# Moving whole parts of the modulation products to other places in a four-layer transformer kernel

## The reference, cut to what matters

```python
mod = jax.nn.silu(c) @ w_mod[l] + b_mod[l]           # (1024,) @ (1024, 6144)
sh1, sc1, g1, sh2, sc2, g2 = jnp.split(mod[:, None, :], 6, axis=-1)
h = x * (1 + sc1) + sh1
x = _layer_norm(ALPHA * x + g1 * mixers(h), ...)
h = x * (1 + sc2) + sh2
x = _layer_norm(ALPHA * x + g2 * mlp(h), ...)
```

## Time and profile before

| | us |
|---|---|
| median of 3 runs | 3222.01 (3219.78 to 3222.47) |
| the profiled execution's own time | 3220.32 |
| its span, first to last instruction | 3219.0 |
| PE busy in the span | 3019.1 (94%) |
| share of PE in the chain that ended last | 87% |
| mean granted clock of TensorE | 0.966 |

### The profile page before, as it was taken

One profiled execution on the slowest core, in us unless ns is written; L12 is line 12 of the kernel. 1 busy time (PEld: TensorE's weight loads), 2 busy tenths in 40 slices (PEclk: granted clock), 3 DMA queues, 4 the chain that ended last, 5 costly groups with the idle time before them and its releaser, 6 DMA issues.

```text
span 3219.0 us, 41567 instructions
## 1 busy us (share of the span) xinstructions
PE 3019.1 (94%) x17128; PEld 2308.4 (72%) x17128; DVE 1418.2 (44%) x2184; ACT 1072.9 (33%) x1807; POOL 313.1 (10%) x334
## 2 busy tenths in 40 slices
PE   5989999999999988999999998997889999899998
PEld 3766657788888866766667776775567888678886
DVE  2556542423233345654444445536734444344443
ACT  3235441412122242553422335212533323342222
POOL 1012220300000030221201002000310000110000
PEclk7999999999999999999999999998989999889999
DMA  6313134222212122103343322422322232222322
GB/s 236 94 58 105 34 119 150 86 99 85 66 60 65 58 77 69 60 14 127 134 150 98 103 87 79 165 94 92 99 85 92 94 96 92 67 66 92 98 92 79
DMA packets 83876, 299.08 MB, mean 93 GB/s; under 512 B 9479, under 2 KB 11783, under 8 KB 83432
## 3 DMA queue, kind: packets, MB, share of 16 engines
q1 hardware_dynamic: 79200, 286.30, 27.2%
q10 hardware_dynamic: 4488, 10.12, 0.9%
HBM read 294.29 MB, written 2.10 MB: 92 GB/s over the span
## 4 chain that ended last, share of the span: by engine, by line
PE 87%; DVE 5%; ACT 4%; issue 2%; DMA 1%; POOL 1%; ACTq 0%; DVEq 0%; POOLq 0%
PE bank L592 42%; PE bank L596 21%; PE bank L1013 4%; PE bank L455 3%; PE bank L1030 3%; PE bank L1074 2%; PE bank L2682 2%; PE bank L1828 1%; PE bank L1566 1%; DMA t<-in_mod 1%; PE bank L1450 1%; PE bank L1022 1%; ACT t L1288 1%; ACT t L843 1%; ACT t L1112 1%
## 5 line engine op out<-in xcount | busy, mean ns | idle before, releaser
L592 PE MATMUL bank<-t 128*128 128x512 f32 (+1 forms) x6432 | 1757.3, 374 | 26.5 <-DVE t L2326 11.1
L592 PEld LDWEIGHTS bank<-t 128*128 128x128 f32 x6432 | 1113.0, 189 | 297.1 <-issue 69.1
L596 PE MATMUL bank<-t 128*128 128x512 f32 (+1 forms) x3216 | 1070.7, 372 | 5.9 <-POOL t L852 5.7
L596 PEld LDWEIGHTS bank<-t 128*128 128x128 f32 x3216 | 556.8, 189 | 127.4 <-POOL t L852 12.0
L486 ACT ACTIVATE t<-t 128x1024 fp32r<-128x1024 f32 x350 | 366.3, 1050 | 558.4 <-PE bank L596 497.5
L496 DVE TENSOR_TENSOR t<-t 128x1024 fp32r<-128x1024 f32 x350 | 430.5, 1234 | 262.4 <-ACT t L486 258.8
L609 DVE SCALAR_TENSOR_TENSOR t<-bank,t 128x512 f32<-128x512 f32 x192 | 129.8, 693 | 511.0 <-PE bank L596 484.2
L933 DVE TENSOR_TENSOR t<-t 128x512 f32<-128x512 f32 (+1 forms) x128 | 98.4, 769 | 335.8 <-ACT t L913 335.8
L913 ACT ACTIVATE t<-bank 128x512 f32<-128x512 f32 (+1 forms) x128 | 83.3, 651 | 418.7 <-PE bank L596 418.7
L1214 POOL TENSOR_SCALAR t<-t 128x768 f32<-128x768 f32 (+3 forms) x160 | 125.7, 788 | 576.3 <-DVE t L1182 576.3
L455 PE MATMUL bank<-t 128*32 128x256 f32 x1536 | 128.9, 414 | 33.7 <-DMA t<-in_mod 23.5
(11 more groups left out here) (289 smaller groups left out, 2281.4 us busy)
## 6 DMA issues: line engine op xcount, KB each, us to landing
t<-in_mod SPq DMA_DIRECT2D x192, 512.0 KB, 4.3
t<-in_l0fc SPq DMA_DIRECT2D x64, 512.0 KB, 3.5
t<-in_l1fc SPq DMA_DIRECT2D x64, 512.0 KB, 3.5
t<-in_s0fc SPq DMA_DIRECT2D x64, 512.0 KB, 3.5
t<-in_s1fc SPq DMA_DIRECT2D x64, 512.0 KB, 3.5
t<-in_mixin SPq DMA_DIRECT2D x24, 512.0 KB, 3.5
t<-in_l0in SPq DMA_DIRECT2D x12, 512.0 KB, 3.6
t<-in_l1in SPq DMA_DIRECT2D x12, 512.0 KB, 3.5
```

Of the source, the lines that this page charges most:

```text
L592: pe.matmul(acc.ap[:, o:o + m], w[:, ws], Hh[:, k, o:o + m], start=k == 0 and w is hi, stop=False)
L596: ins = pe.matmul(acc.ap[:, o:o + m], hi[:, ws], Hl[:, k, o:o + m], start=False, stop=k == NK - 1)
```

## The change

Parts are now placed whole, and at other places:

- Around the norms ln10, ln20, ln11, s0h and pool one part each: 2 tiles before the last pair of sums, 2 before `pe_picks`, 1 before `pe_spread`, 3 behind it.
- In the first two units of the attentions of layers 0 and 1 one part (5, 1 and 2 tiles), and of the differential attention one (5 and 3). In layers 0 and 1 the pieces begin in unit 2 instead of 0.
- Behind the four transforms between layers 1 and 2 one part, at the new mark "transformed".
- In the output projection of layer 0 one mod tile goes behind each weight tile instead of two; in the MLPs of layers 0 and 1 and the output product of the third layer there are none; in the third layer's input products 16 over 20 tiles instead of one behind each, and the row of four is gone. Layer 0's units 4 to 12 have 8 instead of 16.
- The eight tiles of part (3, 5) now stand in a row ahead of the first fc2 tile of the last MLP, where `t.need(L, 5)` places them.
- Turns come earlier in several places (`finish_part`). In the pool layer the first three slices of h are made before the queues' entries up to "pool out".

Counted by part, before and after: (0,3) attention units 4 to 8, now units 0 and 1; (1,3) output projection, now ln10; (1,4) MLP, now ln20; (1,5) MLP, now projections of layer 1; (2,0) these projections, now units 0 and 1 of attention 1; (2,4) MLP, now ln11; (2,5) MLP, now behind the transforms; (3,2) input products and the row of four, now units 0 and 1 of the differential attention; (3,3) that attention, now s0h; (3,4) that attention, now pool; (3,5) output product, now the last MLP.

```diff
+    def spaced(self, n, i, count, upto):
+        self.fill(n * (i + 1) // count - n * i // count, upto)
+
+    def gap(self, tag, counts, upto):
+        assert not any(counts) or not self.pending and self.parts and not self.parts[-1][2], tag
+        for i, n in enumerate(counts):
+            self.fill(n, upto)
+            self.mark(("gap", tag, i))
+        assert sum(counts) in (0, NK), tag
...
-def mlp_order(t, name, L, upto):
+def mlp_order(t, name, L, n, upto, after, counts):
...
-            if m % 4 != 3:
-                t.fill(1, upto)
+            t.spaced(n, 16 * q + m, 64, upto)
...
+    t.finish_part()
     t.mark((name, "end"))
+    t.gap(after, counts, min(upto + 1, 3))
+
+GAP, NO_GAP = (2, 2, 1, 3), (0, 0, 0, 0)
...
-    todo = [(0, x) for x in pair_pieces(l, 0)]
+    todo = [(2, x) for x in pair_pieces(l, 0)]
...
-    mods = ((4, 9, 8), (28, 32, 8)) if l else ((4, 13, 16), (20, 25, 8), (38, 48, 16))
+    mods = ((6, 9, 8), (28, 32, 8)) if l else ((6, 11, 8), (20, 25, 8), (38, 48, 16))
...
+        if u == 1:
+            t.fill(1, l + 1)
         t.mark((f"att{l}", u, "mid"))
         piece(u)
+        if u < 2:
+            t.fill((5, 2)[u], l + 1)
...
-        t.fill(1 if l else 2, l + 1)
+        t.fill(1, l + 1)
+    t.finish_part()
     t.mark((name, "ln1"))
-    mlp_order(t, name, l, l + 1)
+    t.gap(f"ln1{l}", GAP, l + 1)
+    mlp_order(t, name, l, 0, l + 1, f"ln2{l}", NO_GAP if l else GAP)
...
+    t.fill(8, 3)
+    t.mark("transformed")
...
-        t.fill(1, 3)
+        t.spaced(16, n, 20, 3)
...
+    t.finish_part()
     for u in range(16):
-        t.fill(1, 3)
+        if u < 2:
+            t.fill((5, 3)[u], 3)
...
-        t.fill(1, 3)
-    mlp_order(t, "s0", 2, 3)
+    t.gap("s0h", GAP, 3)
+    mlp_order(t, "s0", 2, 0, 3, "pool", GAP)
...
-    mlp_order(t, "s1", 3, 4)
+    t.gap("s1h", NO_GAP, 3)
+    mlp_order(t, "s1", 3, 0, 4, "final", NO_GAP)
...
             if pair == 3:
+                pe_tiles(("gap", N.tag, 0))
             pe_sums(N, pair)
...
+        pe_tiles(("gap", N.tag, 1))
         PEQ.wait_ge(*ps[2].after(("sums", N.tag)))
...
+        pe_tiles(("gap", N.tag, 2))
         PEQ.wait_ge(*at("dve_scales", N.tag))
...
+        pe_tiles(("gap", N.tag, 3))
...
             pe_transform(3)
+            pe_tiles("transformed")
...
             act_transformed(3)
+            act_tiles("transformed")
...
         act_norm_end(N)
+        act_second_h(N, L, 1, work, Hh, range(0, 3))
         act_tiles("pool out")
         act_tiles(("pool", 0))
-        act_second_h(N, L, 1, work, Hh, range(0, 6))
+        act_second_h(N, L, 1, work, Hh, range(3, 6))
...
-        dve_tiles("pool out")
...
         dve_norm_end(N)
+        dve_second_h(N, work, range(0, 3))
         dve_tiles(("pool", 0))
-        dve_second_h(N, work, range(0, 6))
+        dve_second_h(N, work, range(3, 6))
```

More of the change, by code:

```diff
@@ L236, in mlp_order @@
             t.tile((name + "fc2", 8 * q + m))
-            if m % 4 != 3:
-                t.fill(1, upto)
+            t.spaced(n, 16 * q + 8 + m, 64, upto)
+    t.finish_part()
     t.mark((name, "end"))
+    t.gap(after, counts, min(upto + 1, 3))
+GAP, NO_GAP = (2, 2, 1, 3), (0, 0, 0, 0)
 def pair_pieces(l, p):
@@ L285, in first_order @@
         piece(u)
+        if u == 1:
+            t.fill(1, l + 1)
         t.mark((f"att{l}", u, "mid"))
         piece(u)
+        if u < 2:
+            t.fill((5, 2)[u], l + 1)
         for a, b, n in mods:
             if a <= u < b:
-                t.fill(n * (u + 1 - a) // (b - a) - n * (u - a) // (b - a), l + 1)
+                t.spaced(n, u - a, b - a, l + 1)
         if u == 8 * nb - 1:
@@ L669, in pe_norm_step @@
         for pair in ({3: (0,), 5: (1,), 7: (2, 3)} if N.centered else {2: (0,), 4: (1,), 6: (2,), 7: (3,)}).get(m, ()):
+            if pair == 3:
+                pe_tiles(("gap", N.tag, 0))
             pe_sums(N, pair)
```

## The result

| | before | changed |
|---|---|---|
| median of 20 runs each, us | 3220.79 (3215.87 to 3223.15) | 3227.98 (3218.11 to 3237.67) |
| ratio to before, 95% interval | 1 | 1.0023 (1.0014 to 1.0031) |
| profiled execution, us (span) | 3220.32 (3219.0) | 3219.33 (3218.0) |
| mean granted clock | 0.966 | 0.976 |
| PE busy, us | 3019.1 | 3013.4 |

The forecast was 3202, the range 3188 to 3214. It took 3228.67, close to the median, and most readings here are from it.

A forecast was written before the change was run, and what follows sets the result against it. PE bounds the kernel (87% of the wait chain), with mod-tile loads pacing work in pauses. Terms -42.0 - 5.4 + 9.9 + 5.8 + 0.4 + 0.2 + 14 = -17.1, clock 3 more: -20.1, so 3202 us; range 3188 to 3214.

The forecast's parts named there:

- attention 0: Layer 0's attention: unit 2 starts 4.0 us earlier, eight tiles leaving -4.0, four pieces coming in +2.6; net -5.4, between -9 and 0.
- the other places: ln10 +1.8, ln20 +1.7, attention 1 +5.8, ln11 +2.9, transforms +0.2, differential attention +0.4, pool +2.1, last MLP +14 us.
- the clock: Pauses and products behind them: tiles keeping the clock full could return 15 us; 3 taken because load waits leave pauses.
- What went out: Mod tiles leaving busy stretches, 0.77 us each in the MLPs, third-layer output and input products; with layer 0's output projection and row, 42.0.
- a tile's load in a pause: Parts in pauses, three buffers: fourth tile starts 4.3 us after the first; a lone load lands 3.56 after its issue.
- the last MLP: Eight tiles in a row before fc2 end at 11.1 us, then copy, turn and low clock: +14, between +6.2 and +18.
- behind the transforms: Eight tiles from 1980.8 end at 1990.6, before 1991.85: +0.2 us, +3 if a load is late.
- item 3: Rival, chance 0.13: loads land 1 us later at 12 waits, +12, 3214; or removed tiles worth only 0.5 each, 3212.
- Item 4: Rival, chance 0.07: ring turns pauses into load waits, landings 7.79 not 3.56, +50, 3252; decides from 1.7 us later per landing.
- items 1: The forecast itself, chance 0.60: loads of 3.56 us pace each part, 3202 us (3196 to 3208).
- Item 2: Rival, chance 0.20: more work in each pause keeps the clock up, 12 of the 15 us come back, 3193.
- Attention 1: Layer 1's attention: first tile waits for condition vectors, units 0 and 1 cost +3.2, pieces elsewhere +2.6; +5.8, between -3 and +9.

The follow-up runs named there:

- again: Second profile and comparison of the unaltered changed kernel: profiled 3228.67 us, median 3226.93 (9 runs), ratio 1.0023 to the kernel before.
- first profile: First profiled execution of the changed kernel, nothing else altered: 3219.33 us, against 3220.32 for the kernel before.
- the best kernel: Changed kernel plus fourth buffer in two stretches, last MLP's part spread, buffers lent at ln10 and behind the transforms: 3188.20 us, ratio 0.9898 to before.

## Why the prediction was wrong

By the rows of the table: the two MLPs, the output projection, the input products, the row of four and the output product with s0h were to give 40.6, attention 0 5.4, the other places to cost 28.9, and the clock to give 3: -20.1. In *again* they gave 37.3 and 2.8, the others cost 50.0, and the prologue gave 1.4: +8.5.

**What went out was right but for 3.3 us.** A mod tile between weight tiles was 0.77 by the earlier trace rows; the two MLPs gave 11.5 and 10.8 for 16, so 0.72 and 0.68. The kernel without loads gives the same (11.6 and 10.6), so this is PE's own time.

**The step that failed is a tile's load in a pause**: "4.3 from a tile's start to the start of the tile three behind it", with its 3.56 for a landing. From the first tile of a part to its fourth it took, in us:

| | first profile | *again* |
|---|---|---|
| attention 0; ln20 | 4.3; 4.2 | 4.3; 4.3 |
| attention 1; differential attention | 4.6; 4.8 | 4.6; 4.6 |
| transforms; last MLP | 5.0; 5.0 | 4.9; 5.0 |
| pool; s0h | 4.7; 6.1 | 5.5; 5.0 |
| ln11; ln10 | 6.0; 5.9 | 5.4; 7.2 |

It held in attention 0 and at ln20. In these two and in attention 1 the fourth tile's load landed 3.4 to 3.6 us after its issue, in the others 3.9 to 6.4. It failed in three ways.

1. *A full ring was taken for granted.* It is full at ln20, where the weight tiles just before stand without mod tiles, and there the forecast held (+1.7 against 1.5 and 2.1). At ln10 and ln11 the last tile of the part before is done right ahead of the pause, so that the load into the third buffer is issued only 1.0 to 1.2 us ahead of the part's first tile: the third tile waits, then the fourth. That is +5.3 and +6.8 at ln10 where 1.8 was forecast, and 5.7 and 4.9 at ln11 for 2.9. With three buffers lent ln10 costs 0.6 to 0.7.
2. *A round of loads was taken as quicker than it is.* A lone load lands 3.4 to 3.6 us after its issue, but a burst sets free three buffers within a microsecond, and the loads then land 1.3 to 2.5 us behind one another. In attention 0 and the last MLP the forecast had put 1.3 between them; behind the transforms it had left that out. In the last MLP and behind the transforms a weight tile's load was also still in flight, so that the first of the round landed 4.2 us after its issue. So each second round of tiles starts late: in the last MLP the eighth tile came at 13.0 us for 10.3 (+16.9 for 14), behind the transforms the fifth at 7.0 and the end at 14.2 for 9.8 (+4.1 for 0.2). What put 2.5 instead of 1.3 us between two landings isn't shown.
3. *Other traffic was named as a rival and priced too low.* At pool the bands (1152 KB) fly beside the tiles, and the first five loads behind the part's start land 4.7 to 8.0 after their issue; this is worth 1.5 to 2 us there by the kernel with the bands later. By places, what was put into pauses and into the last MLP cost 21.1 us more than forecast (50.0 for 28.9), 1.8 for each of the 12 waits of item 3, which gave 1. Item 4, the other side, had the mechanism ("the ring turns the pauses into load waits"), at 50 us and 0.07, and set its turning point at 1.7 us per wait, so the outcome lies just beyond it; it dismissed it because "at the norms SP has nothing else to issue". What SP had to issue was the part itself.

A slip in the chances changes nothing: all of items 1 and 2 and a third of 3 make 0.84, not 0.86.

**Attention 0** gave 2.8 instead of 5.4, and this isn't loads: without them it is 2.3. Units 0 and 1 gave 4.5 and 4.6 for 4.0. From unit 2 to unit 12, where eight tiles leave and four pieces come in, 1.0 and 0.9 were lost where 1.4 was to be gained. And 1.5 each was lost in units 20 and 21 and in units 30 and 31, whose order is the same in both kernels: there the clock fell, for 3.4 us each. Units 20 and 21, PE's same work before and in *again*:

```profile
308.30:314.74 6.44, 5.14 (x57) 3.44 (x56) 4.50 (x17) 2.97 (x10) 2.98 (x4) 1.00 0.26 84
...
303.76:311.70 7.94, 6.71 (x61) 4.30 (x60) 4.03 (x16) 2.85 (x9) 2.57 (x4) 0.86 0.22 68
```

Both profiles of the changed kernel have these two, the one before neither. PE's pause ahead of the fall is as long in both kernels (1.96 and 1.95 us in unit 20, 1.72 and 1.72 in unit 30), so why the clock falls in one alone is open. About 2 us came back at the end of the attention, where one mod tile is gone and the low clock lasts 3.4 us instead of 6.8. **Attention 1** cost 7.0 to 9.3 for 5.8: its loads are 3.5 to 5.8 of that, since without them it costs 3.5.

**The clock.** Item 2 let added work hold the clock up. The means of the three profiles, 0.976 and 0.973 against 0.966, are no sign of it: the profile before has 44.4 us at the low clock in the prologue (13.0 to 57.4), where nothing was changed and the others have none, and over all runs the medians are 0.971 (20 runs) and 0.973 (*again*, 9 runs) against 0.972 for the kernel before beside the latter (19 runs). Where the load waits stand it is low. Busy time by stretch in *again*, behind the transforms and in the last MLP's burst, then in the best kernel behind the transforms (PEclk third from last):

```profile
1972.04:1988.88 16.84, 8.62 (x74) 3.18 (x73) 7.80 (x10) 8.36 (x13) 4.64 (x4) 0.69 0.76 254
...
2878.30:2893.49 15.19, 7.42 (x68) 2.03 (x67) 1.39 (x2) 2.00 (x4) 0.00 (x0) 0.66 0.60 208
```

```profile
1952.10:1963.69 11.59, 5.09 (x69) 2.83 (x69) 7.24 (x11) 7.44 (x11) 3.81 (x3) 0.87 0.64 228
```

0.69 and 0.66 where PE works off eight tiles with waits between them, 0.87 where seven of them are at hand. Over whole runs it is 0.979 in all five runs of the changed kernel without loads against 0.972 and 0.973 in the kernel before without them, and 0.981 in the best kernel. So item 2's cause holds where its condition (no waits inside the pause) does, and that is what the ring took away; how many of its 12 us come from the clock no run separates.

**The spread** is no noise of the measurement: 19.6 us for the changed kernel with loads, 1.7 without, 4.4 with four buffers, 2.2 in the best (with fewer runs in each of the last three). The two profiles differ in when loads land (the fourth tile's at ln10 5.2 and 6.4 us after its issue) and in where the clock falls (the fence on pool above). Which of the two comes first in a long run is open: the changed kernel has no profile of a run above 3229. With one profile at the fast end of such a kernel, its span says little on the median.

The Trainium skill's page "DMA: Bandwidth & Descriptors" (section "Rules for kernel authors") says to issue a DMA early and wait for it late. The prediction cited this against the change and gave it 0.20 in all; the runs agree with the page, by 44 us. The section "Bandwidth" of the same page of the Trainium skill has two limits, 435 GB/s for the fabric and about 358 GB/s for a core's share of the HBM, and says that for loads from HBM the second binds. Here three loads of 512 KB that land 1.27 us apart move 413 GB/s, on one core; so the measurement stands above the second limit and near the first.

## What to carry to other kernels

A pause of the busiest engine is free room for work only if the work's operands are already there: count how many of its tiles are loaded at the moment the pause begins, not how many buffers the ring has, and price the others as a batch that shares the bandwidth. Work that streams weights through a short ring cost least here where it stood one tile at a time between long ones; to bring it into a pause, first find it memory, if only lent. Between the parts in the pauses with and without memory of their own lie here, with one part spread, 3218 and 3188.

## What was not expected of the hardware

- Loads of 512 KB issued 0.43 us apart, with nothing else under way, landed 3.6, 4.4 and 5.3 us after their issue (2245.08, 2245.51 and 2245.94 in *again*, landing at 2248.67, 2249.95 and 2251.20): 1.27 apart, 413 GB/s.
- Outside the prologue the same load took 3.3 to 8.0 us in one kernel, by what was in flight; the median, 4.3 us before and 4.4 after, doesn't show this.
- A mod tile that finds its weights takes 0.46 us in a burst at the full clock, and 0.72 or 0.68 between weight tiles.
- The granted clock fell to its low level for 3.4 us at two places of attention 0 (302.6 and 360.6 in *again*) where neither the order of the work nor PE's pause just ahead differs from the kernel before, in which it stayed at the full level. Each cost 1.5 us.
